# Causal mask put into the running sums by GpSimd, and the gathered expert rows laid half in the lower and half in the upper partitions

## The reference, cut to what matters

```python
# forgetting attention ("fox"), per head and block of 128 queries
logits = einsum(qb, k) * scale + dq - dcum            # dcum: running sum of log forget gates
logits = where(kpos <= qpos, logits, -inf)            # the causal mask
out = softmax(logits) @ v

# stick-breaking attention ("stick"), per head
z = einsum(qb, k) * scale
after = reverse_cumsum(log_not) - log_not
w = where(kpos < qpos, exp(log_sigmoid(z) + after), 0)

# experts
for e in range(32):
    hid = silu(t @ w_gate[e]) * (t @ w_up[e])
    out += combine[:, e] * (hid @ w_down[e])
```

## Time and profile before

| | |
|---|---|
| median of 3 runs | 710.95 us (710.42 to 713.12) |
| profiled execution | 711.37 us, span 709.5 us |
| PE busy | 690.8 us, 97% of the span |
| DVE, ACT, POOL busy | 373.2, 254.5, 91.3 us |
| chain that ended last | PE 89%, DVE 4%, DMA 3% |
| granted TensorE clock | 0.995 on average |
| HBM read, written | 155.68 MB, 16.00 MB |

### The profile page before, as it was taken

How to read it: one execution, slowest core, us unless ns; L and a number is a source line. 1 busy time by engine, 2 the same in 40 slices (tenths; PEclk the granted TensorE clock), 3 DMA queues, 4 the chain that set the end, 5 groups by cost and what they waited for, 6 DMA issues and landing times.

```text
span 709.5 us, 10025 instructions
## 1 busy us (share of the span) xinstructions
PE 690.8 (97%) x3923; PEld 508.0 (72%) x3923; DVE 373.2 (53%) x732; ACT 254.5 (36%) x423; POOL 91.3 (13%) x130
## 2 busy tenths in 40 slices
PE   8999999999999999999999999999999999999894
PEld 7888988777777777788888888666555556555442
DVE  5378996666676868556446214752513121212227
ACT  7332133587676777544244211220101111111113
POOL 2000922000000101100003000011311312131100
PEclk9999999999999999999999999999999999999998
DMA  7523244322222111493406699699999999999993
GB/s 241 177 61 118 61 127 143 139 75 75 75 75 74 48 59 49 162 385 113 136 2 237 225 382 346 268 353 387 405 417 420 403 419 418 419 419 417 419 394 134
DMA packets 60585, 164.58 MB, mean 232 GB/s; under 512 B 8090, under 2 KB 39911, under 8 KB 48116
## 3 DMA queue, kind: packets, MB, share of 16 engines
q1 hardware_dynamic: 54820, 151.77, 56.3%
q0 software_dynamic: 5712, 12.11, 4.6%
HBM read 155.68 MB, written 16.00 MB: 242 GB/s over the span
## 4 chain that ended last, share of the span: by engine, by line
PE 89%; DVE 4%; DMA 3%; ACT 1%; issue 1%; POOL 0%; SPq 0%; POOLq 0%; DVEq 0%; ACTq 0%
PE psum L1749 31%; PE psum L2175 14%; PE psum L1848 12%; PE psum L2201 8%; PE psum L2028 6%; PE psum L1860 3%; PE psum L2141 2%; DVE ring_e L1105 2%; DMA ring_e<-y_dram 2%; PE psum L1873 1%; PE psum L1904 1%; PE psum L2184 1%; DMA y_dram<-ye,slots_b 1%; PE psum L1987 1%; PE psum L1939 1%
## 5 line engine op out<-in xcount | busy, mean ns | idle before, releaser
L1749 PE MATMUL psum<-xh,wh 128*128 128x512 f32 x256 | 99.9, 390 | 0.8 <-DVE xl L1105 0.8
L1749 PE MATMUL psum<-xl,wh 128*128 128x512 f32 x256 | 99.6, 389 | 0.0
L1749 PE MATMUL psum<-xh,wl 128*128 128x512 f32 x256 | 99.6, 389 | 0.0
L1108 DVE TENSOR_TENSOR wl<-raw,wh 128x1280 fp32r<-128x1280 f32 (+4 forms) x37 | 71.8, 1945 | 24.6 <-ACT wh L801 9.0
L1105 DVE SCALAR_TENSOR_TENSOR hid<-psum,rslot,act_g 128x256 f32<-128x256 f32 x17 | 8.2, 483 | 92.3 <-PE psum L2175 91.7
L1749 PEld LDWEIGHTS psum<-xh,wh 128*128 128x128 f32 x256 | 48.1, 188 | 11.0 <-DVE xl L1105 1.0
L1749 PEld LDWEIGHTS psum<-xh,wl 128*128 128x128 f32 x256 | 48.1, 188 | 10.0
L1749 PEld LDWEIGHTS psum<-xl,wh 128*128 128x128 f32 x256 | 48.1, 188 | 9.8
L1848 PE MATMUL psum<-xh,wh 128*128 128x512 f32 x128 | 51.3, 401 | 0.0
L1848 PE MATMUL psum<-xh,wl 128*128 128x512 f32 x128 | 50.1, 391 | 0.0
L1848 PE MATMUL psum<-xl,wh 128*128 128x512 f32 x128 | 49.9, 390 | 0.0
(11 more groups left out here) (388 smaller groups left out, 1531.6 us busy)
## 6 DMA issues: line engine op xcount, KB each, us to landing
raw<-in_w_gate SPq DMA_DIRECT2D x16, 1024.0 KB, 6.3
raw<-in_w_in SPq DMA_DIRECT2D x9, 1024.0 KB, 5.5
ring_w<-in_w_expert_gate SPq DMA_DIRECT2D x8, 1024.0 KB
ring_w<-in_w_expert_up SPq DMA_DIRECT2D x8, 1024.0 KB
ring_h<-in_w_expert_down SPq DMA_DIRECT2D x8, 1024.0 KB
ring_h<-in_w_expert_gate SPq DMA_DIRECT2D x6, 1024.0 KB
ring_e<-in_w_expert_down SPq DMA_DIRECT2D x6, 1024.0 KB
ring_e<-in_w_expert_gate SPq DMA_DIRECT2D x6, 1024.0 KB
```

The lines of the kernel that those rows point to most:

```text
L1108: return dve.tensor_tensor(dst, src, hi.bitcast(F32), ALU.subtract)
L1749: last = nc.tensor.matmul(dst, a, b, start=start and n == 0, stop=stop and n == len(seq) - 1)
```

## The change

Two things are changed, which share no data.

**The mask of the fox attention.** The tile `maskb` and its matmul (line 1908) are gone. Instead POOL writes 2^100 into `dcum` itself, above the diagonal of the block that the step needs, by an `affine_select` of 128 x 128 in place (`later_keys`); DVE subtracts `dcum` as before. As a masked block stays masked, a head's query blocks now run from the last to the first: `fox_step` gives `qt` = 3, 2, 1, 0. DVE waits for the mask (semaphore `made`), POOL makes the next step's mask when DVE's instruction of this step is done. The semaphore `l_psum` is signalled by the last score product, ahead of the `cutb` product.

**The gathered rows.** `slot_no` now gives the even ranks of an expert to the lower 32 partitions of its 64 and the odd ranks to the upper 32. A second set of indices, `slots_g`, is used for the gathers: the four quarters of 32 partitions take expert halves 0, 1, 1, 0. `x_out` puts the quarters back in the order of the slots, with three instructions instead of one, in all turns but 0, 7 and 8. `slots_g` has its own four small instructions ahead of `toks` in `slot_columns` and its own exchange in `exchange_columns`; `kept_rows` takes the token numbers from `slots` and not from `toks`.

In `fox_step`, POOL's block and DVE's steps, and in `slot_columns`:

```diff
         def fox_step(n):
-            return fox_head(n // NT), n % NT, (n % NT + 1) * P
+            qt = NT - 1 - n % NT
+            return fox_head(n // NT), qt, (qt + 1) * P
...
+        QUAD, GATHERED = SLOT // 2, (0, 1, 1, 0)
...
+            def later_keys(n):
+                h, qt, m = fox_step(n)
+                select(dcum, P, ALU.is_ge, -MASKED, 0, -1, 1, dcum[:, h, m - P:m]).then_inc(S["made"], 1)
+            pool.wait_ge(S["dc_in"], 16)
+            later_keys(0)
             for n in range(STEPS):
                 h, kt, q0 = stick_step(n)
+                if n + 1 < STEPS:
+                    pool.wait_ge(S["l_max"], n + 1)
+                    later_keys(n + 1)
                 if kt == 0:
                     continue
...
-                        base, step = SLOT // 2 * a + 8 * k, 1
+                        base, step = a + 16 * k, 2
...
+                    dve.wait_ge(S["made"], n + 2)
                     st.link(dve.tensor_tensor_reduce(out=lg[:, 0:m], in0=bank[1][:, 0:m], in1=dcum[:, h, 0:m], scale=1.0,
                                                      scalar=-3e38, op0=ALU.subtract, op1=ALU.max, accum_out=sm[:, 0:1]))
...
+                for q, h in enumerate(GATHERED):
+                    part = slice(q * QUAD, (q + 1) * QUAD)
+                    dve.tensor_scalar(slots_g[part, :], table[part, h, :], float(UNUSED), None, ALU.add).then_inc(S["slots_in"], 1)
+                dve.wait_ge(S["slots_in"], n)
+                dve.tensor_scalar(toks[:, 0:NPAIR], slots_g[:, :], 1, None, ALU.arith_shift_right).then_inc(S["idx_ready"], 1)
                 for h in range(2):
                     half = slice(h * SLOT, (h + 1) * SLOT)
                     dve.tensor_scalar(slots[half, 0:NPAIR], table[half, h, :], float(UNUSED), None, ALU.add).then_inc(S["slots_in"], 1)
-                dve.wait_ge(S["slots_in"], n)
-                dve.tensor_scalar(toks[:, 0:NPAIR], slots[:, 0:NPAIR], 1, None, ALU.arith_shift_right).then_inc(S["idx_ready"], 1)
                 dve.tensor_scalar(slots_b[0:SLOT, 0:NPAIR], table[0:SLOT, 1, :], float(UNUSED), None, ALU.add).then_inc(S["slots_in"], 1)
...
```

On PE:

```diff
-                        nc.tensor.matmul(bank[1][:, 0:m], ql[r2:r2 + HD, j2, qt * P:(qt + 1) * P], kl[r2:r2 + HD, j2, 0:m], start=i == 0, stop=i == 2)
+                        last = nc.tensor.matmul(bank[1][:, 0:m], ql[r2:r2 + HD, j2, qt * P:(qt + 1) * P], kl[r2:r2 + HD, j2, 0:m], start=i == 0, stop=i == 2)
+                    last.then_inc(S["l_psum"], 1)
                     nc.tensor.matmul(bank[0][:, q0:q0 + P], identb[:, :], cutb[:, :], start=False, stop=True,
                                      skip_group_check=True).then_inc(S["z_psum"], 1)
-                    nc.tensor.matmul(bank[1][:, m - P:m], identb[:, :], maskb[:, :], start=False, stop=True,
-                                     skip_group_check=True).then_inc(S["l_psum"], 1)
                     gates(BEHIND_SCORES)
```

In `x_out` and `exchange_columns` on DVE:

```diff
-            def x_out(E, b):
-                dve.wait_ge(S["xt_ps"], E * 2 + (b + 1))
-                dve.tensor_tensor(xT[:, 4 * b:4 * b + 4, :], bank[b][:, :].rearrange("p (c s) -> p c s", s=P),
-                                  gffn_p[:, 4 * b:4 * b + 4].unsqueeze(2).to_broadcast([P, 4, P]), ALU.mult).then_inc(S["xe"], 1)
+            def x_out(c, i, b):
+                dve.wait_ge(S["xt_ps"], turn_no(c, i) * 2 + (b + 1))
+                rows = slice(4 * b, 4 * b + 4)
+                if alone(c, i) or isinstance(c, int) and i == 0:
+                    dve.tensor_tensor(xT[:, rows, :], bank[b][:, :].rearrange("p (c s) -> p c s", s=P),
+                                      gffn_p[:, rows].unsqueeze(2).to_broadcast([P, 4, P]), ALU.mult).then_inc(S["xe"], 3)
+                    return
+                to = xT[:, rows, :].rearrange("p c (h a s) -> p c a h s", h=2, a=2)
+                found = bank[b][:, :].rearrange("p (c h a s) -> p c a h s", c=4, h=2, a=2)
+                dve.tensor_tensor(to[:, :, 0, :, :], found[:, :, 0, :, :],
+                                  gffn_p[:, rows].unsqueeze(2).unsqueeze(3).to_broadcast([P, 4, 2, QUAD]), ALU.mult).then_inc(S["xe"], 1)
+                for h in range(2):
+                    dve.tensor_tensor(to[:, :, 1, h, :], found[:, :, 1, 1 - h, :],
+                                      gffn_p[:, rows].unsqueeze(2).to_broadcast([P, 4, QUAD]), ALU.mult).then_inc(S["xe"], 1)
...
+                dve.wait_ge(S["slots_in"], 7)
+                st.link(dve.tensor_copy(slot_f, slots_g[:, :]))
+                exchanged(moved, slot_f, slot_f[:, OVER:OVER + 1], gap)
+                st.link(dve.tensor_copy(slots_g[:, FIXED:NPAIR], slot_f[:, FIXED:NPAIR]))
+                st.link(dve.tensor_scalar(toks[:, FIXED:NPAIR], slots_g[:, FIXED:NPAIR], 1, None, ALU.arith_shift_right))
                 st.link(dve.tensor_copy(slot_f, slots[:, 0:NPAIR]))
...
```

More of the change, by code:

```diff
@@ L128, in hybrid_trunk @@
         neg_one = sb(main, "neg_one", [P], F32R)
-        maskb = sb(main, "maskb", [P], BF16)
         strictb = sb(main, "strictb", [P], BF16)
@@ L287, in hybrid_trunk @@
         slots_b = sb(moe, "slots_b", [NPAIR + 1], I32)
+        slots_g = sb(moe, "slots_g", [NPAIR], I32)
+        toks_k = sb(moe, "toks_k", [KEPT], I32)
         cw_diag = sb(moe, "cw_diag", [2, P])
@@ L653, in _ @@
             for t, v in ((ident, 0.0), (causal, 1.0), (tri_made, -1.0), (one_made, -1.0),
-                         (maskb, 0.0), (cutb, 0.0), (strictb, 1.0), (oneb, 1.0), (eps, EPS)):
+                         (cutb, 0.0), (strictb, 1.0), (oneb, 1.0), (eps, EPS)):
                 st.mark(pool.memset(t[:], v))
@@ L664, in _ @@
             st.mark(select(tri_made, P, ALU.is_ge, 0.0, 0, -1, 1))
-            st.mark(select(maskb, P, ALU.is_ge, MASKED, 0, -1, 1))
             st.mark(select(cutb, P, ALU.is_gt, MASKED, 0, 1, -1))
@@ L669, in _ @@
             st.link(pool.tensor_copy(identb[:, :], ident[:, :]))
-            pool.sem_inc(S["consts"], 1)
+            pool.sem_inc(S["made"], 1)
             evacuated(pool, "ac")
@@ L704, in _ @@
                     for k, d in enumerate((2, 0, 1, 3) if a else (0, 2, 3, 1)):
-                        base, step = SLOT // 2 * a + 8 * k, 1
+                        base, step = a + 16 * k, 2
                         if k % 2:
-                            base, step = base + 7, -1
+                            base, step = base + 14, -2
                         st.mark(pool.iota(lanes[:, h, a, d, :], pattern=[[step, 8]], base=base, channel_multiplier=0, allow_small_or_imprecise_dtypes=True))
@@ L771, in expert_pass @@
                         if i == 0:
-                            pool.wait_ge(S["slots_in"], c * 3 + 3)
+                            pool.wait_ge(S["slots_in"], c * 7 + 7)
                         turn()
@@ L808, in _ @@
                 if t == 0:
-                    act.wait_ge(S["consts"], 1)
+                    act.wait_ge(S["made"], 1)
                 act.activation(stat[:, 1, t:t + 1], stat[:, 0, t:t + 1], ACT.Sqrt, bias=eps[:, 0:1], scale=1.0 / D).then_inc(S["root"], 1)
@@ L1179, in _ @@
             split_lo(1, KC * PROJ[1][2])
-            dve.wait_ge(S["consts"], 1)
+            dve.wait_ge(S["made"], 1)
             st.mark(dve.tensor_copy(causal_r[:, :], causal[:, :]))
@@ L1531, in exchange_columns @@
                 st.link(dve.tensor_scalar(slots[first, OVER:OVER + 1], rs[first, 13, 0:1], float(UNUSED), None, ALU.add))
-                st.mark(dve.tensor_scalar(toks[:, FIXED:NPAIR], slots[:, FIXED:NPAIR], 1, None, ALU.arith_shift_right))
+                st.mark(dve.tensor_scalar(toks[first, OVER:OVER + 1], slots[first, OVER:OVER + 1], 1, None, ALU.arith_shift_right))
                 one_column(bank[7][:, 256:256 + NE], fmask)
@@ L1598, in kept_rows @@
             def kept_rows(k):
-                st.link(dve.tensor_copy(tok_kept[:, k:k + 1], toks[:, NPAIR - KEPT + k:NPAIR - KEPT + k + 1]))
+                kept = NPAIR - KEPT + k
+                st.link(dve.tensor_scalar(toks_k[:, k:k + 1], slots[:, kept:kept + 1], 1, None, ALU.arith_shift_right))
+                st.link(dve.tensor_copy(tok_kept[:, k:k + 1], toks_k[:, k:k + 1]))
                 dve.tensor_scalar(pick[k][:, :], tok_no[:, :], tok_kept[:, k:k + 1], None, ALU.is_equal).then_inc(S["pick_ready"], 1)
@@ L1617, in expert_pass @@
                 for b in range(2):
-                    x_out(turn_no(c, 0), b)
+                    x_out(c, 0, b)
                 if isinstance(c, int):
                     dve.wait_ge(S["slot_ps"], 1)
-                    slot_columns(2, bank[3])
+                    slot_columns(4, bank[3])
                     st.link(dve.tensor_copy(rc[:, 0, :], bank[3][:, 320:320 + NE]))
@@ L1651, in expert_pass @@
                         for b in range(2):
-                            x_out(E + 1, b)
+                            x_out(c, i + 1, b)
                     if isinstance(c, int) and i == 0:
@@ L1728, in _ @@
                     dve.wait_ge(S["rs_ps"], c + 2)
```

(8 more changed lines are left out.)

3 lines of the change are left out of this document (1 added, 2 removed).

## The result

| | before | changed |
|---|---|---|
| median, six runs each | 711.03 us (709.54 to 713.12) | 717.08 us (716.00 to 718.36) |
| ratio, 95% interval | | 1.0077 (1.0055 to 1.0098) |
| profiled execution, span | 711.37, 709.5 us | 717.49, 715.8 us |
| first score product to the first product with `y` behind the stage | 155.08 us | 159.86 us |
| last down product begins at | 686.68 us | 692.89 us |

The forecast was 715.0 us, 0.6% slower; it came out 0.85% slower by the two medians.

A forecast was written before the change was run, and what follows sets the result against it. PE alone was taken to bound the attention stage; in the expert stage PE and transfers ran almost level. 711.37 + 4.5 (attention) - 0.5 (experts) = 715.4 us profiled, median 715.0 us after 0.42 off, range 713.8 to 716.3 us.

The forecast's parts named there:

- Unequal widths, +5.7 us: Attention stage: pairs of unequal width cost 2.2 us more in scores and 3.5 us more in weights times values.
- linear law between 0.55 and 0.96 us: Attention scores: time from first score product to the maskb product, taken as linear between width 128 (0.55) and 512 (0.96).
- rule of the wider member: Attention pairs: the wider member decides, so a head's steps cost widths 512, 384, 384, 512 instead of 128, 256, 384, 512.
- rival of the sum of the widths: Attention: short members let their half run ahead, only summed widths count, so +5.7 becomes 0: 709.2 us, chance 0.08.
- The mask's matmuls, -1.0 us: Attention on PE: the 16 matmuls of line 1908 go, at 0.06 us each, 1.0 us less.
- Selects and DVE's new wait, nothing: Attention: POOL's 16 selects, between 0.3 and 1.7 us each, and DVE's wait for the mask cost nothing.
- The rival with 721.6 us: Attention: a 1.67 us select holds DVE up beyond its 1.26 us of slack, 6.6 us over 16 steps; chance 0.05.
- The stage's end, -0.25 us: End of attention: PE's 0.25 us wait for ACT's pt goes, as pt has 128 columns; between 0 and -0.6.
- The exchange, +1.3 us: Expert stage, turn 2: six added small rows ahead of hid delay PE by 1.3 us early, 0 at the end.
- What comes back at the end: End of expert stage: PE's waits for weights and hid, 1.4 + 0.4 + 1.0 = 2.8 us, can absorb earlier delay.
- The expert stage, -0.5 us: Expert stage in all: near to nothing, taken as -0.5 us, with bounds +1.3 and -1.5 us.
- The rival with -1.5 us from the row order: Expert stage gives back all it can, 2.8 us of waits less 1.3, through faster transfers: 713.9 us, chance 0.18.

The follow-up runs named there:

- e3: Kernel before with only the fox attention's query blocks taken from last to first, mask still a matmul: 716.70 us, ratio 1.0080.
- e8: Kernel before with POOL's mask in the running sums, query blocks first to last, masked blocks restored by transfer from dc_dram: 710.46 us, ratio 0.9983.
- e5: Kernel before with six more linked DVE rows in the exchange ahead of turn 2's hid, gathered rows unchanged: 711.61 us, ratio 1.0009.
- e2: Kernel before with only the change of the gathered rows, attention as before: 712.24 us, ratio 1.0008.
- e6: Kernel before with 24 more linked DVE rows in the exchange ahead of turn 2's hid: 715.80 us, ratio 1.0074.
- e7: Changed kernel with the whole exchange of turn 2 put behind hid and xT instead of ahead of them: 722.38 us, ratio 1.0144.
- e4: Changed kernel with the gather's quarters in plain order 0, 0, 1, 1, every instruction kept: 716.84 us against 717.08 of the changed kernel.
- e11: e10 with the gather's quarters in plain order 0, 0, 1, 1, every instruction kept: 711.24 us, ratio 0.9993.
- e12: e10 run again, on the same chip and beside the same runs of before as e11: 708.99 us, ratio 0.9970.
- e1: Kernel before with only the attention's change (POOL mask, query blocks last to first), gathered rows as before: 717.61 us, ratio 1.0090.
- e10: e8 plus the gathered rows' change, with turn 2's exchange split so only rows the turn 4 gather needs precede hid: 709.43 us, ratio 0.9972.

## Why the prediction held, point by point

- **Unequal widths, +5.7 us: right.** Scores +2.32 us (forecast 2.2) and weights times values +3.37 us (3.5). The linear law between 0.55 and 0.96 us and the rule of the wider member stand, shown by e3 with the order alone. The wider member's passes follow at the distances that the forecast named as its sign, 0.23 us for 128 with 512 (144.80 to 145.03) and 0.17 us for 256 with 384 (153.35 to 153.52). The rival of the sum of the widths saw its mechanism, the short member running ahead, and not its effect.
- **The mask's matmuls, -1.0 us: right.** 1.52 to 0.62 us, 0.90 less. e8 keeps this and drops the cost.
- **Selects and DVE's new wait, nothing: right.** 0.293 us each, no wait. The rival with 721.6 us falls; the row with the same instruction was the right one, not the one of four times the columns. Nor does the port rule of the Trainium skill (SBUF — State Buffer, "SBUF: two separate sides") show any effect in these 16 selects; with so little DVE work beside 15 of them they hardly test it.
- **The stage's end, -0.25 us: too much.** With a `pt` of 128 columns the wait went from 0.25 to 0.17 us only. The sum for the stage is +4.78 us against +4.5.
- **The exchange, +1.3 us: right**, 1.33 us in its rows, 1.43 at the down product; and e5 shows a delay of this size coming back whole, as forecast. But one reading was wrong: PE's wait of 1.6 us for `hid` does not stand in turn 2, where it is 0.49 us (503.29), but ahead of the last down product (684.40). The forecast used it for both places. That PE waits for `hid` in turn 2 at all was enough for the exchange to count in full.
- **What comes back at the end: mis-sized.** The forecast let the exchange use up 1.3 us and bounded the rest by 2.8 us of waits. The cap was right within 0.2 us: the changed kernel, e2, e6 and e7 each got 3.0 us back. Its 1.0 us of `hid` is the wait of the last turn (1.64 to 0.69 us). I took only a small part of it, because I expected PE to lose 1.3 us inside the stage and not 4.3.
- **The expert stage, -0.5 us: the step that failed.** It came out at +1.3 us (4.9 us late on entry, 6.2 at the last down product), at the far bound. It left out the clock. The forecast named the exchange's wait and asked only what it delays, not what a longer idle stretch of PE does to the rate behind it. In e4 that is 1.5 us, and in e5's runs at 0.993 and 0.994 the median is 711.7 against 710.9 us. In the profiled execution of the changed kernel it was the long fall in turn 1 instead, 2.9 us. What set off that one is not shown: kernels without the change have it by their mean clock too, so this part of the miss may be chance.
- **The rival with -1.5 us from the row order: masked.** Its mechanism exists (e11 and e12, 2.2 us between the medians), but it needs PE to wait for transfers, and the changed kernel had lost 4.3 us inside the stage, more than its waits can give back. The 4.9 us on entry don't do that: e1 enters 5.6 us late and waits for weights as before. e4, with the plain order, takes the same time as the changed kernel.

The rest of the way from 715.0 to 717.08 us is then 0.3 us of the attention and 1.8 us of the expert stage.

## What to carry to other kernels

Two streams that share the array in halves cost what the wider member of each pair costs, so the order of one must not be changed without the other's. A gain in transfers is only seen where the consumer waits for them; test it in a version in which nothing else makes the consumer late. And a few small linked instructions ahead of a matmul's operand cost their sum once, but an idle stretch of PE that they lengthen can cost as much again in the clock behind it: move out what the next reader doesn't need, and leave what an early transfer needs. Both together made e10 the best version here, 709.43 and 708.99 us in two jobs, 0.3% below the kernel before.

## What the runs showed of the hardware that I had not expected

- Passes on different halves of the array start out of program order: stick's third at 144.73 us, fox's second, which stands before it, at 144.80.
- The granted clock fell to its lower level for some 7 us with PE busy throughout the stretch before it (6.00 of 6 us, and 7.00 of 7 in e2). 70 of 85 runs of before have a mean clock of 0.995 or more, and its profile has no fall there. Why it falls in one run and not in another stays open; PE's rows before the fall are those that the profile of before has at the same place of the program.
- Whether the long fall is more frequent with the gathered rows (changed, e2, e4: 8 of 22 runs; before: 15 of 85) can't be settled with so few runs.
